# The second product of the Hyena filter's output layer over 128 rows instead of 64

## The reference, cut to what matters

```python
HY_FILT_HIDDEN = 64
"hy_filt_w_out_2": nrm((nB, HY_FILT_HIDDEN, HY_ORDER * 2 * HY_WIDTH), 0.005)
```

## Time and profile before

| | |
|---|---|
| median of three runs | 2823.53 us (2819.08 to 2827.93) |
| span of the profiled execution, first to last instruction | 2809.8 us |
| between that span and the median | 13.7 us |
| PE busy in the span | 2609.7 us, 93% |
| DVE busy in the span | 1857.7 us, 66% |
| mean granted clock of PE | 0.960 |
| first stage, in which the change lies | 0 to 347 us of the span |

### The profile page before, as it was taken

How to read it: one execution, slowest core, us unless ns; L and a number is a source line. 1 busy time by engine, 2 the same in 40 slices (tenths; PEclk the granted TensorE clock), 3 DMA queues, 4 the chain that set the end, 5 groups by cost and what they waited for, 6 DMA issues and landing times. The chain is left out here.

```text
span 2809.8 us, 31107 instructions
## 1 busy us (share of the span) xinstructions
PE 2609.7 (93%) x11373; PEld 1866.5 (66%) x11373; DVE 1857.7 (66%) x3035; ACT 1005.7 (36%) x1839; POOL 935.6 (33%) x668
## 2 busy tenths in 40 slices
PE   7999989988899998999999999989999997999977
PEld 2444468885555676777878999977788883444355
DVE  6677499997886556578407777756844417887454
ACT  2122257504344434554345555544322210011132
POOL 0000022381332566766332313146422212331244
PEclk8999989998999998999999999999999998999988
DMA  5112201210012232457463121134211125111053
GB/s 191 64 72 90 93 29 38 69 66 9 16 61 91 97 113 80 138 203 269 157 224 88 46 79 56 51 109 161 86 50 45 45 83 187 47 33 49 30 195 105
DMA packets 100937, 260.90 MB, mean 93 GB/s; under 512 B 9410, under 2 KB 28876, under 8 KB 96306
## 3 DMA queue, kind: packets, MB, share of 16 engines
q1 hardware_dynamic: 100786, 258.91, 27.3%
HBM read 200.10 MB, written 58.78 MB: 92 GB/s over the span
## 5 line engine op out<-in xcount | busy, mean ns | idle before, releaser
L313 PE MATMUL psum<-part,part 128*128 128x512 f32 (+1 forms) x2176 | 842.2, 387 | 38.4 <-POOL part L2002 18.5
L2002 POOL TENSOR_TENSOR part<-arena,part 128x512 fp32r<-128x512 f32 (+1 forms) x322 | 457.2, 1430 | 1145.7 <-ACT part L1996 1145.4
L314 PE MATMUL psum<-part,part 128*128 128x512 f32 (+1 forms) x2176 | 819.0, 376 | 0.0
L315 PE MATMUL psum<-part,part 128*128 128x512 f32 (+1 forms) x2176 | 817.1, 375 | 0.0
L313 PEld LDWEIGHTS psum<-part,part 128*128 128x128 f32 x2176 | 415.4, 191 | 131.6 <-POOL part L2002 32.5
L315 PEld LDWEIGHTS psum<-part,part 128*128 128x128 f32 x2176 | 415.0, 191 | 80.5
L314 PEld LDWEIGHTS psum<-part,part 128*128 128x128 f32 x2176 | 415.8, 191 | 79.0 <-issue 2.9
L1996 ACT ACTIVATE part<-arena 128x512 fp32r<-128x512 f32 (+1 forms) x322 | 195.9, 621 | 317.8 <-PE psum L315 258.4
L3320 PE MATMUL psum<-arena 128*128 128x512 f32 x448 | 192.9, 592 | 0.0
L2842 DVE TENSOR_REDUCE arena<-psum 128x1 f32<-128x1280 f32 x64 | 95.4, 1491 | 102.3 <-PE psum L2794 102.3
L3320 PEld LDWEIGHTS psum<-arena 128*128 128x128 f32 x448 | 85.1, 190 | 107.1 <-issue 107.1
(11 more groups left out here) (340 smaller groups left out, 4190.3 us busy)
## 6 DMA issues: line engine op xcount, KB each, us to landing
arena<-in_ada_w SPq DMA_DIRECT2D x24, 1024.0 KB, 5.6
arena<-in_w_hy SPq DMA_DIRECT2D x40, 512.0 KB, 3.5
scratch_spec<-arena SPq DMA_DIRECT2D x68, 256.0 KB, 2.0
arena<-scratch_spec SPq DMA_DIRECT2D x12, 1024.0 KB, 5.2
arena<-in_w_gate SPq DMA_DIRECT2D x16, 512.0 KB, 3.3
arena<-in_w_out SPq DMA_DIRECT2D x16, 512.0 KB, 3.4
arena<-in_w_mgate SPq DMA_DIRECT2D x16, 512.0 KB, 3.9
arena<-in_w_mout SPq DMA_DIRECT2D x16, 512.0 KB, 4.0
```

The costliest lines, as they stand in the source:

```text
L313: nc.tensor.matmul(acc, a_hi, b_hi, start=start, stop=False)
L314: nc.tensor.matmul(acc, a_hi, b_lo, start=False, stop=False)
L315: return nc.tensor.matmul(acc, a_lo, b_hi, start=False, stop=stop)
L2002: self.K.nc.gpsimd.tensor_tensor(self.lo[s][:, c], self.raw[s][:, c], self.hi[s][:, c].bitcast(F32), ALU.subtract).then_inc(self.split, 1)
```

## The change

The rest of the weights is taken in all 128 rows, and the second product of each pair takes 128 rows too. Rows 64 to 127 add the hidden values' rest times the weights' rest, a term that was left out before. Nothing is moved: each engine has the same instructions in the same order, and only the shapes of L877 (64 matmuls and their 64 loads) and of L641 (two instructions) differ. The waits are the same.

```diff
             def rest_of_weights(h):
                 dve.wait_ge(w_rounded, h + 1)
-                v.tensor_tensor(w_lo[h][0:64, :, :, :], w_ed[0:64, h, :, :, :], w_hi[h][0:64, :, :, :].bitcast(F32),
-                                ALU.subtract).then_inc(w_split, 1)
+                v.tensor_tensor(w_lo[h], w_ed[:, h, :, :, :], w_hi[h].bitcast(F32), ALU.subtract).then_inc(w_split, 1)
...
                     mm(acc, hid[:, c], w_hi[h][:, o, s, :], start=True, stop=False)
-                    last = mm(acc, hid[0:64, c], w_lo[h][0:64, o, s, :], start=False, stop=True)
+                    last = mm(acc, hid[:, c], w_lo[h][:, o, s, :], start=False, stop=True)
```

## The result

| | before | changed |
|---|---|---|
| median of five runs | 2819.08 us (2810.41 to 2827.93) | 2793.31 us (2791.71 to 2801.26) |
| ratio | | 0.9917, 95% interval 0.9899 to 0.9935 |
| span of the profiled execution | 2809.8 us | 2790.5 us |
| first matmul of the second stage | 347.3 us | 325.7 us |
| from there to the end of the span | 2462.5 us | 2464.8 us |

The kernel became faster by 0.83%, some 23 us (18 to 28 by the interval). The forecast was 2807.5 us with a range of 2799 to 2816: the sign was right, 2793.31 lies under the range. Of the kernel with bursts A alone, one of ten runs took 6952.91 us at a mean granted clock of 0.515, and it is left out of the ratio.

What follows compares the result with a forecast made beforehand. PE's chain was taken to bound the first stage; burst gains of 14.6 us, corrected by +2.6 and -1.2, made 16 us. Span 2809.8 became 2793.8, plus 13.7 around it 2807.5 us, range 2799 to 2816.

Steps and rivals of the forecast that it cites:

- the price of a bare load: First stage, L876/L877 pairs: a load of differing height isn't started under the running product; 0.20 us each at full clock.
- The first rival: L876/L877 pairs: the load stays bare for a reason unrelated to height; gain 0, 2823.5 us; chance 5%.
- step 0, B: Calls 2 and 3 of step 0, at half clock: 2.3 us earlier, of which 1.15 us remains.
- step 1, A and B: All four calls of step 1, where PE waits for nothing: 1.6 us per burst, 3.2 us.
- steps 2, 3 and 4, A: Calls 0 and 1 of these steps, ahead of PE's waits for L700: gain 0, turned into wait.
- step 2, B: Calls 2 and 3 of step 2, on the path: about 2 us less, half lost to half clock, 1.0 us.
- step 3, B: Calls 2 and 3 of step 3: 2.3 us less, half given back to half clock, 1.15 us.
- steps 5 and 6, A and B: All calls of steps 5 and 6, PE without a wait: 1.1, 1.4, 1.6 and 1.3, together 5.4 us.
- step 7, A and B: All calls of step 7: calls 0 and 1 give 0 as PE waits for DVE, calls 2 and 3 1.35 us.
- the clock term: First stage: half clock ends some 3 us sooner in three places, 0 to +5.1 us, half taken: +2.6 us.
- The second correction: First stage: PE's longer waits might bring a new half-clock stretch at the third, 0 to -3.4 us; taken as -1.2 us.
- My fourth rival: PE's four waits for L700: longer waits bring 51 us of half clock, 25 lost; slower, 2834 us; chance 2%.

Runs made afterwards that it cites:

- bursts A alone: Changed kernel with 128 rows in the second product only in calls 0 and 1 of each step, 64 in calls 2 and 3; ratio to before 1.0013.
- bursts B alone: Changed kernel with 128 rows in the second product only in calls 2 and 3 of each step, 64 in calls 0 and 1; ratio to before 0.9929.
- early rounding: Changed kernel with ACT rounding the second half's weights in step 1 between its two parts, not in step 2; median 2784.85 us, ratio to before 0.9888.

## Why the prediction was wrong in size

**Right: the price of a bare load.** 0.43 to 0.23 us at full and 0.72 to 0.43 at half clock, and that a change of height lays the load bare and not 64 rows by themselves. All these products start at row 0, so what a change of position does at equal height was not tried. The first rival (no gain, as the row groups don't differ) is refuted twice, at 128 and at 64 rows.

**Mostly right: the path.** What each burst gave, by how much earlier the next hand-over came than before:

| burst | forecast, without the two corrections | measured |
|---|---|---|
| step 0, B | 1.15 | 3.4 |
| step 1, A and B | 3.2 | 3.1 |
| steps 2, 3 and 4, A | 0 | 0 |
| step 2, B | 1.0 | 3.2 |
| step 3, B | 1.15 | 3.7 |
| step 4, B | 1.35 | 1.4 |
| steps 5 and 6, A and B | 5.4 | 6.2 |
| step 7, A and B | 1.35 | -0.5 |
| sum, before rounding | 14.6 | 20.45 |

(21.6 less 1.15 that lay ahead of the first burst.) Burst A of step 7 takes back 0.4 of what step 6 gave, in PE's longer wait for DVE, and burst B of step 7 met a new half-clock stretch at 264.9, which ate its 1.35. The forecast of the waits themselves was right in one of four: I let each grow by what the burst ahead of it gives, to 4.9, 7.3, 2.7 and 0.5 us, and they measured 4.87, 4.00, 1.56 and 2.29. The second shrank because PE lost its time before it comes to that wait: the groups ahead of it, here before and after, wait 1.4 us longer for DVE's fold, and the new half-clock stretch at 128.4 makes them 1.7 us longer, against 1.3 that the burst gives.

```profile
138.51 8.85 PE L885 MATMUL psum<-arena 128*128 128x512 f32 x20 [0.60 <-DVEq L422]
127.66 10.55 PE L884 MATMUL psum<-arena 128*128 128x512 f32 x20 [1.98 <-DVEq L422]
```

That is why the stretch at 128.4 cost nothing: it came out of a wait.

**Wrong: the clock term, the first of the two corrections.** I let half clock end "some 3 us sooner" in three places and took half of the worth, +2.6, with a ceiling of +5.1. The three bursts that lay in half clock gave 10.2 us in place of 3.3, so by the difference the term measured +6.9: the stretches behind the two waits shrank by 3.4 and 6.9 us, and the one at the start by 3.4, and these 13.7 us at half speed are 6.8 us of work. Two things failed in it: taking half of it without a reason, and the 3 us, which was 6.9 behind the wait of step 3. The kernels with bursts B alone and with bursts A alone go the same way, 27.3 against 47.8 us of half clock, but each is one profile. Over whole runs, the mean granted clock was 0.9603 in 24 later runs of before and 0.9626 in the five of the changed kernel; the difference of 0.0023 is some 6 us of a run (an estimate from these means). In the stage alone, the profiles have 6.8 to 10.2 us less of half clock, 3.4 to 5.1 us of work. Why half clock ended so much sooner behind bursts without bare loads stays open.

The second correction, -1.2 for new stretches, was about right in size (-1.35) and wrong in place: nothing at 172.7, where I had looked for it, but at 264.9; the one at 128.4 lay ahead of a wait. My fourth rival, that longer waits cost more than the loads give, did not happen in the changed kernel; the one with bursts A alone looks like a small case of it, by the clock of its nine runs.

**Wrong: the base.** I added 13.7 us to the span as what lies around it. A run's time is its span plus 1.8 us in every run that lists both (2792.33 and 2790.5, 2807.03 and 2805.2). So the profiled execution of before took about 2811.6, and the other 11.9 us were the distance of that run from a median of three high runs; later series of before gave medians of 2815 (14 runs) and 2818 (9 runs). With the right 1.8 my own sum says 2795.6 for an execution like the profiled one, and the changed kernel's profiled run took 2792.33.

Of the 14.2 us between 2807.5 and 2793.3, 4.4 are the median of before, which fell from 2823.53 to 2819.08 with two more runs; the other 9.8 are a gain of 25.8 between medians where I had 16. Against the 24 later runs of before, with a median of 2815.6, the gain is 22.3. By the first two profiles it was 19.3: my 16, then 4.3 that the clock term lacked, 0.8 in steps 5 and 6, less 0.4 at burst A of step 7 and 0.2 elsewhere, 1.15 ahead of the first burst, and less 2.3 behind the stage. The last two are what executions differ by. The spread of before (2806.5 to 2828) goes in good part with the clock: of those 24 runs the slowest, 2827.18, has a mean granted clock of 0.957, and 2806.76 has 0.963. In which stages that sits was not settled; behind the first stage, the profiles of all kernels here range from 2458.6 to 2469.8 us.

## What to carry to other kernels

Where products of different heights alternate on PE, look at whether a load starts with its own matmul or with the one before; if with its own, each change of height costs 0.20 us at full clock. Padding the short product to the full height removes all changes and was free here, where the extra rows held data that may be added and the wider L641 took no longer; grouping by height removes half of them. Then ask of each faster stretch who is released behind it: the bursts behind a wait gave 11.6 of the 20.45 us, those of steps 1, 5 and 6, where PE doesn't wait, gave 9.3, those ahead of a wait gave nothing, and step 7 took back 0.5. And read what lies between a span and a run's time from one and the same run, never from a median of others.

## What the runs showed of the hardware that I had not expected

- Products of 64 rows, at the same distances of 0.23 us, left half clock standing: 44.4 us in the stage, against 23.9 to 27.3 with 128 rows and 34.1 to 47.8 with bare loads. Each of the 64-row cases is one profile, and kernels with the same work on PE differ by 13.7 us in this, so that the height is the reason is not shown.
- Filling PE's waits with unread products took half clock from about 25 to 6.8 us, and from 17.1 to 0 with early rounding, but gave only 3 to 5 us of a stage of 290, where half of the half clock that went would be some 9 us. Part of it probably lay beside DVE's work; that was argued from the lists and not measured.
- PE's loads cost 0.18 to 0.19 us for 64 rows as for 128.
